# Taking eight unused columns off a small scratch tensor, so that every tensor laid behind it moves by 32 bytes

## The chip, the cores and the metric

The kernel runs on one core of a Trainium2 chip. The metric is the device time in microseconds (us) of one execution, as the median of several runs. The time before the change is 1901.88 us (three runs, 1901.18 to 1902.07).

## The reference

One layer of an encoder on 256 tokens of width 2048, in float32. Shortened:

```
x = x + 0.5 * swiglu_ffn(x, ffn1_norm, ffn1_w_in, ffn1_w_out)      # 2048 -> 2 x 5632 -> 2048
proj = rms_norm(x, mix_norm) @ w_in                                # 2048 -> 6144
# 8 heads of dilated attention and 8 heads of differential attention on proj
mixed = concatenate([a_o, b_o])
x = x + mixed @ w_out                                              # 2048 -> 2048
x = x + 0.5 * swiglu_ffn(x, ffn2_norm, ffn2_w_in, ffn2_w_out)

def swiglu_ffn(x, g, w_in, w_out):
    gate, up = split(rms_norm(x, g) @ w_in)
    return (silu(gate) * up) @ w_out
```

## The kernel before

All five big products have one form. The 256 tokens are held transposed, with the contraction in the 128 partitions, as TensorE's stationary operand. The weights stream from HBM through `w_raw` and are the moving operand, 512 columns at a time. To keep float32 accuracy, each operand is held as two parts, a rounded one (`_hi`) and the rest (`_lo`), and each product is three matmuls: line 330 multiplies the activations' `_hi` with `w_hi`, line 331 the same with `w_lo`, and line 332 the activations' `_lo` with `w_hi`. ScalarE makes `w_hi` from `w_raw` (line 531), VectorE makes `w_lo` from `w_raw` and `w_hi` (line 734), in a ring of four slots, so that TensorE, ScalarE and VectorE follow each other by semaphores.

The stationary operand is `h_hi`/`h_lo` for the up-projections of both feed-forward parts and for `w_in`; it is `act_hi`/`act_lo` for both down-projections, and `mix_hi`/`mix_lo` for `w_out`. In time: first feed-forward part to 794 us (its down-projection from 506 us), `w_in` with the attention of earlier heads slipped between its matmuls, `w_out` from about 1058 us, then the second feed-forward part, whose down-projection ends the kernel.

`inverse_root` (lines 744 to 760) computes 1/sqrt on VectorE by an integer estimate and three Newton steps. Its scratch tensor is `root`: the mean goes to columns 0 to n, a square to 16 to 16 + n, the bits to 32 to 32 + n, and n is at most 16.

How the tensors lie in on-chip memory matters for this change. They are laid one behind another in each partition, in the order in which the code asks for them, each start rounded up to a multiple of 32 bytes; `act_hi`, `act_lo` and the attention's tensors share one region, since they live at different times. Worked out from the shapes, with the first tensor `x_sb` at byte 1152:

| tensor | starts at byte | remainder by 128 |
|---|---|---|
| `rows` | 17536 | 0 |
| `h_hi`, `h_lo` | 33920, 50304 | 0 |
| `w_raw`, `w_hi`, `w_lo` | 66688, 99456, 115840 | 0 |
| `cst` | 132224 | 0 |
| `rstd`, `lam`, `root` | 138784, 138816, 138848 | 32, 64, 96 |
| `act_hi`, `act_lo` | 139072, 184128 | 64 |
| `mix_hi`, `mix_lo` | 139072, 155456 | 64 |
| `qkv` | 171840 | 64 |
| `qk_t`, `w_t` | 210752, 212800 | 64 |
| `head_ss`, `head_rstd` | 215872, 215904 | 64, 96 |
| `qk_ss`, `qk_rstd` | 217472, 217536 | 0, 64 |

Slices of `act`, `mix` and `h` that TensorE loads are 512 bytes long and lie at multiples of 512 bytes from the tensor's start.

Inside the attention, GpSimd multiplies and rotates queries and keys (lines 1005 to 1014), and TensorE transposes and multiplies per head (lines 414, 427, 436, 448).

Of the kernel before, what the change touches and what calls it, by code (L numbers as in the profile page):

```python
# [25 lines left out]
P = 128  # L26
# [81 lines left out]
def hybrid_layer_kernel(nc, x, ffn1_norm, ffn1_w_in, ffn1_w_out, mix_norm, w_in, a_q_norm, a_k_norm, b_q_norm,  # L108
# [8 lines left out]
    with ExitStack() as ctx:  # L117
        def sb(name, shape, dt=F32, stack=ctx):
            return stack.enter_context(nc.sbuf_tensor(name, shape, dt))
# [16 lines left out]
        sumsq = sb("sumsq", [P, TT, 4])  # L136
        rstd = sb("rstd", [P, TT])
        lam = sb("lam", [P, 4])
        root = sb("root", [P, 56])


        with ExitStack() as hidden:
# [893 lines left out]
```

How the kernel before makes its waits and increments, by code:

```python
        def wait_read(eng, stage, q):  # L236
            b, before = place(stage, q)
            eng.wait_ge(bank_free[b], READS[stage][b] + before + 1)
# [20 lines left out]
        @block.sync  # L260
# [1 line left out]
            def load(src, col, k0, count, p, j):  # L262
                if not isinstance(p, int) or p >= RAW:
                    sp.wait_ge(lo_ready, (p - RAW + 1) * 2)
                sp.dma_start(w_raw[:, j % RAW, 0:count, :],
                             src[:, k0:k0 + count, bass.ds(col, NC)]).then_inc(raw_landed[j % RAW], 16)
# [5 lines left out]
            def ffn(w1, w2, s_in, s_out, started, gain, norms):  # L273
                gate_up = tiled(w1)
                with sp.Fori(started, FFN_ITERS) as i:
                    load_chunk(gate_up, i * NC, PARTS_D, i * 8 + PIECE[s_in])
                    load_chunk(gate_up, i * NC + FF, PARTS_D, i * 8 + PIECE[s_in] + 4)
                if gain is not None:
                    sp.wait_ge(rows_ready, norms)
                    sp.dma_start(gain_row[:, :], gain.to_broadcast([P, D])).then_inc(gain_landed, 16)
                down = tiled(w2)
                with sp.Fori(0, 4) as n:
                    load_chunk(down, n * NC, PARTS_F, n * len(PARTS_F) + PIECE[s_out])
# [22 lines left out]
                for kind in range(3):  # L306
                    load_chunk(qkv_w, base + kind * (D // 2), PARTS_D, PIECE[QKV] + SEG * g + 4 * kind)
            sp.wait_ge(rows_ready, ROWS[R_MIX])
            sp.dma_start(gain_row[:, :], ffn2_norm.to_broadcast([P, D])).then_inc(gain_landed, 16)
```

## Time and profile before

| what | value |
|---|---|
| median of 3 runs | 1901.88 us |
| profiled execution, its own time | 1901.88 us |
| its span, first to last instruction | 1899.8 us |
| mean granted clock of TensorE | 0.998 of full speed |
| TensorE busy | 1878.3 us, 99% of the span |
| VectorE busy | 1021.0 us, 54% |
| ScalarE busy | 857.3 us, 45% |
| GpSimd busy | 60.1 us, 3% |
| traffic | 352.86 MB, mean 186 GB/s |

The span is what the trace can be asked about; the profiled execution's own time is 2.1 us more. A matmul's duration in the profile overlaps with that of the next, because the engine is a pipeline. How fast TensorE goes is therefore read from the distance between the starts of matmuls that follow each other, not from the duration of one.

### The profile page before, as it was taken

The page shows a single profiled execution, that of the slowest core. Times are in us where ns is not written, and L with a number is a line of the kernel's source. Part 1 is how long each engine was busy: PE and PEld are TensorE (multiplying, and loading weights), DVE is VectorE, ACT ScalarE, POOL GpSimd, SP SyncE. Part 2 cuts the span into 40 slices and gives each one's busy share as a digit, 9 for nine tenths or more (in the row PEclk, how much of TensorE's full clock was granted, in tenths as well). Part 3 has the DMA queues.
Part 4 walks back from the last instruction along what each step waited for, and adds up shares of the span by engine and source line. Part 5 has one row for each costly group of instructions (what it writes and reads, how often), then busy time and mean ns, then how long its engine had stood idle before and what let it go on. Part 6 is the DMA issues. An engine that isn't in the chain of part 4 may idle for free.

```text
span 1899.8 us, 22606 instructions
## 1 busy us (share of the span) xinstructions
PE 1878.3 (99%) x8528; PEld 1553.5 (82%) x8528; DVE 1021.0 (54%) x1142; ACT 857.3 (45%) x1063; POOL 60.1 (3%) x60
## 2 busy tenths in 40 slices
PE   7999999999999999999999999999999999999999
PEld 6888888888888888877888788888888888888887
DVE  5544445444544554667777666444444454444443
ACT  5444444444434444555555554444444444433342
POOL 0000000000000000122021100000000000000000
PEclk9999999999999999999999999999999999999999
DMA  8555555555655565554545355555555555555563
GB/s 304 187 191 191 184 197 180 197 182 193 207 188 173 190 201 191 183 190 137 178 155 184 127 171 179 183 198 180 195 186 189 192 184 197 180 180 186 198 206 116
DMA packets 178135, 352.86 MB, mean 186 GB/s; under 512 B 6561, under 2 KB 7201, under 8 KB 177825
## 3 DMA queue, kind: packets, MB, share of 16 engines
q1 hardware_dynamic: 177936, 352.07, 54.3%
q8 instruction: 35, 0.57, 0.1%
q14 instruction: 20, 0.16, 0.0%
q10 hardware_dynamic: 144, 0.07, 0.0%
HBM read 350.01 MB, written 2.10 MB: 185 GB/s over the span
## 4 chain that ended last, share of the span: by engine, by line
PE 94%; DVE 3%; ACT 1%; issue 1%; POOL 1%; DMA 0%; SPq 0%; ACTq 0%
PE acc L330 30%; PE acc L332 30%; PE acc L331 30%; DVE w_lo L734 1%; PE turn L357 1%; PE turn L427 1%; PE turn L448 1%; DMA w_raw<-in_ffn_w_in 0%; ACT w_hi L531 0%; PE turn L332 0%; PE turn L330 0%; PE turn L331 0%; ACT probs L621 0%; PE turn L436 0%; PE turn L414 0%
## 5 line engine op out<-in xcount | busy, mean ns | idle before, releaser
L734 DVE TENSOR_TENSOR w_lo<-w_raw,w_hi 128x1024 fp32r<-128x1024 f32 (+1 forms) x672 | 821.2, 1227 | 845.6 <-ACT w_hi L531 844.1
L531 ACT ACTIVATE w_hi<-w_raw 128x1024 fp32r<-128x1024 f32 (+1 forms) x672 | 697.2, 1040 | 974.8 <-PE acc L332 952.5
L330 PE MATMUL acc<-w_hi,h_hi 128*128 128x512 f32 x1792 | 703.2, 392 | 1.9 <-DVE w_lo L734 1.9
L332 PE MATMUL acc<-w_hi,h_lo 128*128 128x512 f32 x1792 | 698.3, 390 | 0.0
L331 PE MATMUL acc<-w_lo,h_hi 128*128 128x512 f32 x1792 | 698.1, 390 | 0.0
L330 PEld LDWEIGHTS acc<-w_hi,h_hi 128*128 128x128 f32 x1792 | 336.9, 188 | 73.3 <-issue 4.9
L332 PEld LDWEIGHTS acc<-w_hi,h_lo 128*128 128x128 f32 x1792 | 336.8, 188 | 70.4
L331 PEld LDWEIGHTS acc<-w_lo,h_hi 128*128 128x128 f32 x1792 | 337.0, 188 | 68.6
L330 PE MATMUL acc<-w_hi,act_hi 128*128 128x512 f32 x704 | 277.2, 394 | 0.0
L332 PE MATMUL acc<-w_hi,act_lo 128*128 128x512 f32 x704 | 276.0, 392 | 0.0
L331 PE MATMUL acc<-w_lo,act_hi 128*128 128x512 f32 x704 | 273.7, 389 | 0.0
L332 PEld LDWEIGHTS acc<-w_hi,act_lo 128*128 128x128 f32 x704 | 132.2, 188 | 30.3
L331 PEld LDWEIGHTS acc<-w_lo,act_hi 128*128 128x128 f32 x704 | 132.2, 188 | 29.4
L330 PEld LDWEIGHTS acc<-w_hi,act_hi 128*128 128x128 f32 x704 | 132.3, 188 | 26.7
L1005 POOL TENSOR_TENSOR qkv<-qkv,gains 128x1024 f32<-128x1024 f32 x8 | 26.5, 3306 | 992.6 <-DVE qkv L853 992.6
L357 PE MATMUL turn<-cst,rows 128*128 128x128 f32 x272 | 37.1, 281 | 8.8 <-DVE rows L773 8.8
L357 PEld LDWEIGHTS turn<-cst,rows 128*128 128x128 f32 x272 | 33.0, 145 | 13.3 <-issue 7.9
L330 PE MATMUL acc<-w_hi,mix_hi 128*128 128x512 f32 x96 | 39.9, 415 | 0.0
L332 PE MATMUL acc<-w_hi,mix_lo 128*128 128x512 f32 x96 | 38.4, 400 | 0.0
L331 PE MATMUL acc<-w_lo,mix_hi 128*128 128x512 f32 x96 | 38.1, 397 | 0.0
L782 DVE SCALAR_TENSOR_TENSOR rows<-acc,rstd,rows 128x512 f32<-128x512 f32 x44 | 30.9, 743 | 0.0
L550 ACT ACTIVATE rows<-acc,rstd 128x512 f32<-128x512 f32 x44 | 27.5, 674 | 0.0
(88 smaller groups left out, 594.6 us busy)
## 6 DMA issues: line engine op xcount, KB each, us to landing
w_raw<-in_ffn_w_in SPq DMA_DIRECT2D x176, 1024.0 KB, 4.9
w_raw<-in_ffn_w_out SPq DMA_DIRECT2D x64, 1024.0 KB, 5.0
w_raw<-in_w_in SPq DMA_DIRECT2D x48, 1024.0 KB, 5.2
w_raw<-in_ffn_w_out SPq DMA_DIRECT2D x32, 768.0 KB, 4.2
w_raw<-in_w_out SPq DMA_DIRECT2D x16, 1024.0 KB, 5.0
x_sb<-in_x SPq DMA_DIRECT2D x4, 512.0 KB, 7.9
out_y<-x_sb SPq DMA_DIRECT2D x4, 512.0 KB, 6.4
gain_row<-in_ffn_norm SPq DMA_DIRECT2D x4, 256.0 KB, 8.5
```

Source lines behind the costliest of these rows:

```text
L330: nc.tensor.matmul(o, hi, w_hi[:, slot, kk, :], start=first and kk == 0, stop=False)
L331: nc.tensor.matmul(o, hi, w_lo[:, slot, kk, :], start=False, stop=False)
L332: mm = nc.tensor.matmul(o, lo, w_hi[:, slot, kk, :], start=False, stop=last and kk == count - 1)
L357: mm = nc.tensor.transpose(turn4[pair][:, k, t * P:(t + 1) * P], rows[:, buf, t, k * P:(k + 1) * P], ident)
L427: mm = nc.tensor.matmul(score[:, c, t, :], qk_t[part, 0, t * P:(t + 1) * P], qk_t[part, 1, :], start=True, stop=True)
L448: mm = nc.tensor.matmul(head_acc[:, t, :], w_t[:, kt, t * P:(t + 1) * P], qkv[:, g % 2, 2, kt, n * HD:(n + 1) * HD], start=kt == 0, stop=k ...
L531: nc.scalar.activation(w_hi[:, v % RING, 0:count, :], w_raw[:, v // 2 % RAW, k0:k0 + count, :], ACT.Copy).then_inc(hi_ready, 1)
L550: s = nc.scalar.activation(rows[:, 0, t, :], acc[0][:, t, :], ACT.Silu, scale=rstd[:, t:t + 1])
L734: nc.vector.tensor_tensor(w_lo[:, v % RING, 0:count, :], w_raw[:, v // 2 % RAW, k0:k0 + count, :], w_hi[:, v % RING, 0:count, :].bitcast(F32),
L782: s = nc.vector.scalar_tensor_tensor(rows[:, 0, t, :], acc[1][:, t, :], rstd[:, t:t + 1], rows[:, 0, t, :], ALU.mult, ALU.mult)
L1005: link(nc.gpsimd.tensor_tensor(whole, whole, gain.unsqueeze(1).to_broadcast([P, TT * heads, width]), ALU.mult))
```

## The change

`root` gets 48 columns in place of 56. Columns 48 to 55 are read and written by nothing. Everything that is asked for behind `root` starts 32 bytes earlier. `act_hi` and `mix_hi` start at byte 139040, `act_lo` at 184096, `mix_lo` at 155424, `qkv` at 171808, `w_t` at 212768. No instruction is added, removed or moved.

```
         rstd = sb("rstd", [P, TT])
         lam = sb("lam", [P, 4])
-        root = sb("root", [P, 56])
+        root = sb("root", [P, 48])
```

## Rows read from the trace of the kernel before

**Rows 1.** The page's first part: busy time, share of the span, instructions.

```profile
PE 1878.3 (99%) x8528; PEld 1553.5 (82%) x8528; DVE 1021.0 (54%) x1142; ACT 857.3 (45%) x1063; POOL 60.1 (3%) x60
```

**Rows 2.** The chain that ended last, its shares by line.

```profile
by line: PE acc L330 29.8%; PE acc L332 29.7%; PE acc L331 29.6%; DVE w_lo L734 1.5%; PE turn L357 1.5%; issue 0.7%; PE turn L427 0.6%; PE turn L448 0.6%; DMA w_raw<-in_ffn_w_in 0.5%; ACT w_hi L531 0.5%; PE turn L332 0.4%; PE turn L330 0.4%
```

**Rows 3.** Waits over the whole kernel: total us, times, longest us.

```profile
ACT w_hi L531 <- PE acc L332: 952.5, 615, 3.6
DVE w_lo L734 <- ACT w_hi L531: 844.1, 581, 6.7
```

**Rows 4.** TensorE in order of time, up-projection: first and last of 19 starts.

```profile
460.17 0.39 PE L330 MATMUL acc<-w_hi,h_hi 128*128 128x512 f32 x1
...
464.25 0.39 PE L330 MATMUL acc<-w_hi,h_hi 128*128 128x512 f32 x1
```

**Rows 5.** The same, first down-projection: first and last of 22 starts.

```profile
599.77 0.39 PE L330 MATMUL acc<-w_hi,act_hi 128*128 128x512 f32 x1
...
604.58 0.39 PE L330 MATMUL acc<-w_hi,act_hi 128*128 128x512 f32 x1
```

**Rows 6.** The same, second down-projection: first and last of 22 starts.

```profile
1834.75 0.39 PE L330 MATMUL acc<-w_hi,act_hi 128*128 128x512 f32 x1
...
1839.56 0.39 PE L330 MATMUL acc<-w_hi,act_hi 128*128 128x512 f32 x1
```

**Rows 7.** The same, output projection: first and last of 9 starts.

```profile
1101.98 0.39 PE L330 MATMUL acc<-w_hi,mix_hi 128*128 128x512 f32 x1
...
1103.81 0.39 PE L332 MATMUL acc<-w_hi,mix_lo 128*128 128x512 f32 x1
```

**Rows 8.** Groups by line and shape: line 330's matmuls, and its weight loads (PEld).

```profile
L330 PEld LDWEIGHTS acc<-w_hi,h_hi 128*128 128x128 f32 x1792 | 336.9, 188 | 73.3 <-issue 4.9
...
L330 PE MATMUL acc<-w_hi,act_hi 128*128 128x512 f32 x704 | 277.2, 394 | 0.0
...
L330 PEld LDWEIGHTS acc<-w_hi,act_hi 128*128 128x128 f32 x704 | 132.3, 188 | 26.7
...
L330 PE MATMUL acc<-w_hi,mix_hi 128*128 128x512 f32 x96 | 39.9, 415 | 0.0
...
L330 PE MATMUL turn<-w_hi,mix_hi 128*128 128x512 f32 x32 | 12.9, 403 | 0.0
```

**Rows 9.** The same view, VectorE and ScalarE on tensors with different starts.

```profile
L536 ACT ACTIVATE h_hi<-turn 128x1024 fp32r<-128x1024 f32 x12 | 12.1, 1011 | 8.7 <-PE turn L357 8.7
...
L536 ACT ACTIVATE mix_hi<-turn 128x1024 fp32r<-128x1024 f32 x4 | 4.0, 1008 | 0.0
...
L754 DVE SCALAR_TENSOR_TENSOR root<-root 128x16 f32<-128x16 f32 x12 | 2.1, 176 | 0.4
L755 DVE SCALAR_TENSOR_TENSOR qk_rstd<-root,qk_rstd 128x16 f32<-128x16 f32 x12 | 2.1, 175 | 0.4
...
L755 DVE SCALAR_TENSOR_TENSOR qk_rstd<-root,qk_rstd 128x8 f32<-128x8 f32 x12 | 2.0, 167 | 0.4
...
L755 DVE SCALAR_TENSOR_TENSOR head_rstd<-root,head_rstd 128x8 f32<-128x8 f32 x9 | 1.5, 167 | 0.3
```

**Rows 10.** Stretches around the end of `w_in`: busy time per engine, granted clock.

```profile
1048.00:1056.00 8.00, 5.51 (x25) 4.21 (x23) 5.83 (x6) 3.32 (x10) 6.09 (x7) 0.99 0.40 126
1056.00:1063.00 7.00, 6.21 (x20) 5.26 (x21) 1.86 (x3) 2.59 (x5) 0.00 (x0) 0.53 0.44 157
```

**Rows 11.** The timeline of the same stretch.

```profile
1047.33 3.31 POOL L1005 TENSOR_TENSOR qkv<-qkv,gains 128x1024 f32<-128x1024 f32 x1 [12.04 <-DVE qkv L853]
1048.30 3.42 DVE L734 TENSOR_TENSOR w_lo<-w_raw,w_hi 128x1024 fp32r<-128x1024 f32 x1
...
1053.12 0.39 PE L332 MATMUL acc<-w_hi,h_lo 128*128 128x512 f32 x1
...
1056.79 1.11 PE L436 MATMUL turn<-cst,probs 128*128 128x128 f32 x4 [3.28 <-DVE row_inv L879]
```

**Rows 12.** The chain in order of time: one matmul behind that stop.

```profile
1060.04 0.43 PE acc L330
```

## Prediction

> **What bounds the kernel now.** I read the page's first part, then the chain, then the waits, and last the matmuls in order of time. The first part shows TensorE busy for 1878.3 of 1899.8 us, VectorE for little more than half of the span [rows 1]. A share of 99% could still hide short waits, so the chain comes next: three lines, 330 to 332, carry 89.1% of it [rows 2]. The waits say the same from the other side. ScalarE waited 952.5 us for TensorE to give a ring slot back, and VectorE 844.1 us for ScalarE; TensorE is on neither left side [rows 3]. So outside a few places in the attention the time is the number of matmuls times the distance between their starts, and only what changes that distance, or stops TensorE, can change the time.
>
> That distance differs by stage, although the matmuls have the same shape. With `h` as the stationary operand it is (464.25 - 460.17)/18 = 226.7 ns [rows 4]. With `act` it is (604.58 - 599.77)/21 = 229.0 ns, in the second feed-forward part again (1839.56 - 1834.75)/21 = 229.0 ns [rows 5, 6]. With `mix` it is (1103.81 - 1101.98)/8 = 228.8 ns [rows 7]. The excess is 2.3 ns for each matmul. The moving operand, the clock and the pace of the other engines are the same. What differs is where the stationary operand lies: `h` begins at a multiple of 128 bytes, `act` and `mix` 64 bytes past one, and they also lie in the upper part of the memory. The trace can't tell these two readings apart, and the change bears on the first alone.
>
> **The change part by part.** It removes no instruction, adds none and adds no wait: 0 us. Columns 48 to 55 of `root` have no reader or writer, since n is at most 16 and the last slice ends at 48: 0 us. What is left is the move by 32 bytes, which takes everything behind `root` from a multiple of 64 to 32 past one. `w_raw`, `w_hi`, `w_lo`, `h`, `rows`, `x_sb` and `cst` lie ahead of it and stay. So the up-projections and `w_in` keep their 226.7 ns, and the weights' DMAs, `w_hi` and `w_lo` are as before.
>
> *TensorE's loads of `act` and `mix`.* The down-projections have 3 x 704 = 2112 such matmuls, the output projection 3 x (96 + 32) = 384, together 2496 [rows 8]. If the 2.3 ns come from the start 64 bytes past a multiple of 128, they are worth 2496 x 2.3 ns = 5.7 us now. A start 32 bytes past could keep that step, lose it, or pay a second one. The bounds are therefore -5.7 us and +5.7 us. I take 0. A load takes 188 ns from `h` as from `act` [rows 8], so the start of 64 past doesn't show in the load's own record, and it has 229.0 - 188 = 41 ns before it would reach the next matmul. Were a load cut into eight pieces of 64 bytes, a ninth, which the new start would touch, would cost 188/8 = 23.5 ns, inside these 41. If it weren't hidden it would cost 2496 x 23.5 ns = 58.7 us. I leave that out of the range, because the operand's present start shows a step of a tenth of that at most.
>
> The Trainium skill ("TensorE: Matmul & The Clock Gate", Step-by-step: what each phase is for) says that TensorE reads SBUF by two independent ports, one for the moving operand and one for weight loads, so that a load takes nothing from a running matmul. By it the place of `act` can't matter while a load fits behind a matmul, and the sum would be 0 for the move, as I take it; but the 2.3 ns above are a difference that it doesn't account for. The Trainium skill ("SBUF — State Buffer", Operand start alignment) asks only that an operand start at a multiple of its element's size, and says that its runs timed nothing.
>
> *ScalarE, VectorE and GpSimd.* Their reads and writes of `act`, `mix` and the attention's tensors move as well. The nearest rows compare starts that differ. ScalarE writes `h_hi` (remainder 0) in 1011 ns and `mix_hi` (64) in 1008. VectorE takes 176 ns for `root` into `root` (96, so 32 past a multiple of 64) and 175 for `qk_rstd`, a multiple of 64; at eight columns `head_rstd` (96) and `qk_rstd` (64) take 167 ns each [rows 9]. No large tensor shows a start 32 bytes past a multiple of 64, so these small ones are the only rows on it, and they say 0. A slowdown here would first be taken up by the 952.5 and 844.1 us of waiting above [rows 3]. That cover is gone in the attention, at one place above all.
>
> *The stop at the end of `w_in`.* GpSimd's multiplication of `qkv` at 1047.33 takes 3.31 us, and `w_lo` beside it 3.42 us. TensorE starts its last matmul at 1053.12 and the next work at 1056.79 [rows 11]. Behind this stop the granted clock is 0.53 of full speed from 1056 to 1063, and 0.99 in the stretch ahead [rows 10]; matmuls start 0.43 us apart at the lower level (1.2 GHz) [rows 12] and 0.23 us at the upper one (2.4 GHz) [rows 4]. The clock row gives about 0.47 x 7 = 3.3 us lost to it. With the same durations this comes back unchanged, so 0 us. If the cover is gone, GpSimd's longer work lengthens the stop one for one, and what is late next is the transposes of line 436 and everything behind them.
>
> Sum: 0 + 0 + 0 = 0 us against the profiled execution's span of 1899.8 and its own time of 1901.88, which is also the median. The forecast is 1901.9 us.
>
> **The rivals.**
>
> *No gain, a second step (slower).* The loads of `act` and `mix` begin 32 past a multiple of 64, each 512-byte slice now ends in the middle of such a piece, and the distance grows by the same 2.3 ns again. For it: the existing excess goes with a start that is no multiple of 128, and 32 is the smaller alignment. Against it: the load's 188 ns don't differ between 0 and 64. Time: 1901.9 + 5.7 = 1907.6. It decides from 1.5 ns for each matmul on (3.8 us over 2496).
>
> *The step falls away (faster).* The excess belongs to the particular distance between the stationary and the moving operand's places, which is 64 by remainder now and 32 after. Then `act` and `mix` could run at 226.7 ns, and 5.7 us are won: 1896.2. Nothing in the rows speaks for 32 being better than 64; only that both distances are unlike zero.
>
> *The stop moves.* An attention engine that is a few tens of ns slower or faster on moved tensors shifts the stop at 1053, and the fall of the clock behind it vanishes (-3.3 us, to 1898.6) or a second one appears at another attention stop (+3.3 us, to 1905.2). For it: one such fall is there. Against it: no row shows a duration that depends on the start.
>
> *The change does nothing at all.* Had the rounding of starts swallowed the eight columns, nothing would have moved. But 32 bytes are just one rounding unit and `root` ends at 139040, so `act_hi` does move. It gives the same time as the forecast.
>
> **How the numbers follow.** A measurement of this kernel can tell about 0.2%, 3.8 us, from no change: the three runs spread over 0.9 us. No change in time, with `act` and `mix` at 229 ns: 0.60. Second step: 0.23. Step gone: 0.10. Stop moved: 0.07, with 0.03 slower and 0.04 faster, taken as just over the bound together with small shifts. That makes faster 0.14, same 0.60, slower 0.26. The range reaches to the second step with a little more for the clock, 1909, and down to the step gone, 1896. Outside are dearer straddling loads and both effects together, under 2 in 10. The likeliest case alone would be 1900.5 to 1903.5.
>
> **What would show it.** In the changed profile the instruction counts are those of [rows 1]. Right is a distance of 229 ns in the down-projections and in the output projection, and 226.7 in the up-projections, where nothing moved; weight loads at 188 ns; one fall of the clock, near 1056. A distance of 231 ns or more, or 227 or less, in the down-projections proves the alignment rivals, and then the up-projections must not have changed. If the distance is the same and the time isn't, the stops in the attention are the place to look. The prediction is wrong if a start 32 bytes past a multiple of 64 costs any engine on TensorE's path more than 1.5 ns for each of its 2496 operations.

## The result, and the profile after

The changed kernel takes 1914.14 us (median of 4 runs, 1910.89 to 1914.24), the kernel before in the same comparison 1901.91 us (4 runs). The ratio is 1.0058, with a 95% interval of 1.0046 to 1.0070: 0.6% slower. The forecast was no change, and the time lies above the stated range.

The profiled execution of the changed kernel has a span of 1908.7 us, 8.9 us more than before. The same 22606 instructions are there. First the page's busy times, which answer to [rows 1]:

```profile
PE 1887.2 (99%) x8528; PEld 1551.3 (81%) x8528; DVE 1021.0 (53%) x1142; ACT 857.5 (45%) x1063; POOL 60.1 (3%) x60
```

The waits, as in [rows 3]:

```profile
ACT w_hi L531 <- PE acc L332: 962.0, 615, 2.2
DVE w_lo L734 <- ACT w_hi L531: 853.2, 588, 4.0
```

TensorE is busy for 8.9 us longer, which is the whole difference. VectorE, ScalarE and GpSimd are busy as long as before to within 0.2 us. ScalarE waits 9.5 us longer for TensorE, and VectorE 9.1 us longer for ScalarE. So no engine became slower but TensorE. Next, TensorE's matmuls in order of time, in the up-projection (22 starts shown by first and last), the first down-projection (23), the end of the output projection (47) and the second down-projection (23), as in [rows 4 to 7]:

```profile
459.73 0.39 PE L332 MATMUL acc<-w_hi,h_lo 128*128 128x512 f32 x1
...
464.49 0.39 PE L332 MATMUL acc<-w_hi,h_lo 128*128 128x512 f32 x1
...
599.68 0.40 PE L332 MATMUL acc<-w_hi,act_lo 128*128 128x512 f32 x1
...
604.81 0.39 PE L330 MATMUL acc<-w_hi,act_hi 128*128 128x512 f32 x1
...
1157.05 0.40 PE L331 MATMUL acc<-w_lo,mix_hi 128*128 128x512 f32 x1
...
1167.78 0.39 PE L332 MATMUL acc<-w_hi,mix_lo 128*128 128x512 f32 x1
...
1834.74 0.39 PE L330 MATMUL acc<-w_hi,act_hi 128*128 128x512 f32 x1
...
1839.88 0.39 PE L331 MATMUL acc<-w_lo,act_hi 128*128 128x512 f32 x1
```

With `h` the distance is 4.76/21 = 226.7 ns, as before. With `act` it is 5.13/22 = 233.2 and 5.14/22 = 233.6 ns, where it was 229.0. With `mix` it is 10.73/46 = 233.3 ns. The same 47 starts in the kernel before:

```profile
1153.09 0.39 PE L331 MATMUL acc<-w_lo,mix_hi 128*128 128x512 f32 x1
...
1163.62 0.40 PE L332 MATMUL acc<-w_hi,mix_lo 128*128 128x512 f32 x1
```

They are 10.53/46 = 228.9 ns apart. A start is read to 0.01 us, so a distance over some 22 matmuls is good to about 0.5 ns.

The weight loads' own record says nothing of it. In the groups by line and shape a load from `act` takes 188 ns, exactly as in [rows 8], and the ScalarE and VectorE groups of [rows 9] are the same to within 1 ns too:

```profile
L330 PEld LDWEIGHTS acc<-w_hi,act_hi 128*128 128x128 f32 x704 | 132.2, 188 | 31.6
...
L536 ACT ACTIVATE mix_hi<-turn 128x1024 fp32r<-128x1024 f32 x4 | 4.0, 1008 | 0.0
...
L754 DVE SCALAR_TENSOR_TENSOR root<-root 128x16 f32<-128x16 f32 x12 | 2.1, 176 | 0.4
```

Is it TensorE alone, or do the other engines' and the DMAs' accesses to the memory get in its way? The last 28 matmuls of the kernel answer this, since nothing else is left to do. In the changed kernel the stretch has (busy PE, PEld, DVE, ACT, POOL, then the granted clock and the DMA share):

```profile
1897.50:1903.80 6.30, 6.30 (x28) 5.07 (x27) 0.00 (x0) 0.00 (x0) 0.00 (x0) 1.00 0.00 0
```

The 28 starts from 1897.51 to 1903.81 are 6.30/27 = 233.3 ns apart. In the kernel before, the last 28, from 1888.77 to 1894.95, are 6.18/27 = 228.9 ns apart, again with the others idle. So the extra time is there with no other engine and no DMA at work beside TensorE.

The lengths of the stages, each from its first big matmul to that of the next stage:

| stage | before, us | changed, us | difference |
|---|---|---|---|
| first up-projection | 491.4 | 491.9 | +0.4 |
| first down-projection | 245.2 | 249.9 | +4.7 |
| `w_in` with attention | 307.2 | 306.5 | -0.6 |
| `w_out` | 105.4 | 105.1 | -0.3 |
| second up-projection | 488.7 | 488.7 | 0.0 |
| second down-projection, to the last matmul | 242.4 | 247.1 | +4.7 |

Each down-projection carries 4.7 us, or 4.4 ns for each of 1056 matmuls. The two stages in the middle are a little shorter although `mix` is slower, because TensorE's clock didn't fall there in this execution. The same stretches as in [rows 10], with one column each for busy PE, PEld, DVE, ACT, POOL, then the granted clock:

```profile
1048.00:1056.00 8.00, 8.00 (x41) 6.79 (x40) 7.56 (x17) 3.33 (x8) 3.33 (x2) 1.00 0.45 158
1056.00:1063.00 7.00, 3.75 (x22) 2.94 (x21) 4.83 (x7) 4.13 (x8) 3.44 (x6) 1.00 0.46 151
```

The stop is there, only later, and the clock stays at 2.4 GHz behind it (1.00). In the timeline, TensorE starts the last matmul ahead of it at 1058.41 and the next work at 1062.06, 3.65 us, against 3.67 in [rows 11]:

```profile
1058.41 0.39 PE L332 MATMUL acc<-w_hi,h_lo 128*128 128x512 f32 x1
...
1062.06 0.66 PE L436 MATMUL turn<-cst,probs 128*128 128x128 f32 x4 [3.25 <-DVE row_inv L879]
```

That fall of the clock comes and goes from one execution to the next of the same kernel. Further executions of the changed kernel lie at 1911 to 1912.5 us, where the mean granted clock is 0.999 or 1.000, and near 1914 us, where it is 0.998. The kernel before, run 14 times in a later comparison, spreads from 1898.96 to 1902.27 us.

### The profile page after: what moved, and what is told of

It reads as the page before. It is cut to its first block, busy times and chain, and to the rows that moved or that the text cites. A ratio compares the mean times of both kernels' runs of the same rounds, so it can differ in the third digit from the quotient of the medians.

```text
span 1908.7 us, 22606 instructions
## 1 busy us (share of the span) xinstructions
PE 1887.2 (99%) x8528; PEld 1551.3 (81%) x8528; DVE 1021.0 (53%) x1142; ACT 857.5 (45%) x1063; POOL 60.1 (3%) x60
## 4 chain that ended last, share of the span: by engine, by line
PE 94%; DVE 3%; ACT 1%; issue 1%; POOL 1%; DMA 0%; SPq 0%; ACTq 0%
PE acc L332 30%; PE acc L331 30%; PE acc L330 30%; DVE w_lo L734 1%; PE turn L357 1%; PE turn L427 1%; PE turn L448 1%; DMA w_raw<-in_ffn_w_in 0%; ACT w_hi L531 0%; PE turn L332 0%; PE turn L331 0%; PE turn L330 0%; ACT probs L621 0%; PE turn L436 0%; DVE qk_ss L846 0%
## 5 line engine op out<-in xcount | busy, mean ns | idle before, releaser
L332 PE MATMUL acc<-w_hi,act_lo 128*128 128x512 f32 x704 | 280.6, 399 | 0.0
```

Source lines behind the costliest of these rows:

```text
L332: mm = nc.tensor.matmul(o, lo, w_hi[:, slot, kk, :], start=False, stop=last and kk == count - 1)
```

## Experiments

All kernels differ from the kernel before only in where tensors lie: in unused columns, and in one case also in the place of `cst` in the order. The theories' letters are those of the expectations. D below is the start of the stationary operand (`h`, `act` or `mix`) less the start of the moving one (`w_hi`), modulo 256 bytes, written from -96 to 128. The `_lo` tensors have the same remainder as their `_hi` partners unless said. The kernel before has D = 0 for `h` and -64 for `act` and `mix`; the changed one has -96 for the latter.

**First group: is it the stationary operand's own place?**

72 columns in `root`, so `act` and `mix` start at a multiple of 128 bytes:

```
-        root = sb("root", [P, 56])
+        root = sb("root", [P, 72])
```

> `root` has 72 columns, so `act` and `mix` start at a multiple of 128 bytes, like `h`, still in the upper part of the memory. Theory A (the start of the stationary operand by 128 bytes sets the distance between matmuls): the distance with `act` falls from 229.0 to 226.7 ns, and the time by 2496 x 2.3 ns = 5.7 us to about 1896. Theory C (the excess of 2.3 ns comes with the upper part of the memory, and only 32 bytes off a multiple of 64 costs extra): 229.0 ns and 1901.9 us. Theory D (the loss sits in the attention's tensors, not in `act` and `mix`): 229.0 ns in the down-projections.

Measured 1896.85 us (10 runs) against 1901.65 (14 runs), ratio 0.9975 (0.9965 to 0.9984). The down-projection in order of time, 23 starts:

```profile
599.81 0.39 PE L330 MATMUL acc<-w_hi,act_hi 128*128 128x512 f32 x1
...
604.80 0.39 PE L331 MATMUL acc<-w_lo,act_hi 128*128 128x512 f32 x1
```

4.99/22 = 226.8 ns: the excess of `act` over `h` is gone. The place was its cause, not the upper part of the memory (theory C falls), and not the attention's tensors (theory D falls). This version beats both kernels.

The same with 64 columns:

> `root` has 64 columns, so `act` and `mix` start 96 bytes past a multiple of 128: again 32 past a multiple of 64, but shifted the other way than in the changed kernel. Theory A with a fold by 64: the same 233.3 ns as the changed kernel and 1911 to 1914 us. If the two halves of 128 bytes differ: something between 229.0 and 233.3 ns, or more. Theory C: 233.3 ns.

Measured 1911.37 us (4 runs), ratio 1.0052 (1.0037 to 1.0068). 5.13/22 = 233.2 ns in the down-projection, the changed kernel's distance.

Eight columns between `act_hi` and `act_lo`:

```
+            pad = sb("pad", [P, 8], F32, hidden)
             act_lo = sb("act_lo", [P, KF, SEQ], F32R, hidden)
```

> The kernel before with eight unused columns between `act_hi` and `act_lo`: only `act_lo` moves, to 96 past a multiple of 128; `mix` and the attention stay. Theory A, each load pays for itself: one load of three is dearer, so the distance rises by a third of the 4.4 ns, to about 230.4 ns, and the time by 2112 x 1.5 ns = 3.1 us to 1905. If the extra comes only where two neighbouring loads have different starts, it is more than a third. If it is the attention's tensors that cost: no change, 1901.9.

Measured once, 1909.88 us, with 5.13/22 = 233.2 ns. One moved load in three costs as much as three. So a load doesn't pay for itself; the reading that each of the 2496 loads has a price of its own is wrong.

Sixteen columns ahead of `w_hi`:

```
+        pad = sb("pad", [P, 16])
         w_hi = sb("w_hi", [P, RING, UK, NC], F32R)
```

> The kernel before with 16 unused columns ahead of `w_hi`: `w_hi` and `w_lo` start 64 past a multiple of 128, `act` and `mix` at a multiple of 128, `h` stays at a multiple. Theory A (only the stationary operand counts): `h` 226.7 ns, `act` 226.7 ns, about 1896 us. Theory B (the place of the stationary operand relative to the moving one counts): `h` rises to 229.0 ns and `act` stays at 229.0, so 5376 x 2.3 = 12 us slower, 1914.

Measured once, 1910.80 us. The up-projection, 23 starts:

```profile
459.81 0.39 PE L331 MATMUL acc<-w_hi,h_hi 128*128 128x512 f32 x1
...
464.85 0.39 PE L332 MATMUL acc<-w_lo,h_hi 128*128 128x512 f32 x1
```

`h` hasn't moved, and its matmuls are 5.04/22 = 229.1 ns apart in place of 226.7. `act`, now at a multiple of 128, has 5.03/22 = 228.6. The stationary operand's own place (theory A) explains neither.

**Second group: the distance between both operands?**

Both moved by 64 bytes against `h`:

```
+        pad = sb("pad", [P, 16])
         w_hi = sb("w_hi", [P, RING, UK, NC], F32R)
...
-        root = sb("root", [P, 56])
+        root = sb("root", [P, 72])
```

> `w_hi` and `w_lo` start 64 past a multiple of 128 and so do `act` and `mix`; `h` stays at a multiple of 128. Theory B (only the distance between the two operands' places counts): `act` 226.7 ns, `h` 229.0. Theory E (each operand's own start counts, and the worse of the two sets the pace): `h` 229.0 and `act` 229.0, about 1911 us. Theory F (the costs of the two operands add up): `act` 231.2 ns, about 1916.

Measured once, 1908.09 us. The down-projection (24 starts):

```profile
599.78 0.39 PE L332 MATMUL acc<-w_lo,act_hi 128*128 128x512 f32 x1
...
604.99 0.39 PE L331 MATMUL acc<-w_hi,act_hi 128*128 128x512 f32 x1
```

`act` 5.21/23 = 226.5 ns, `h` 5.27/23 = 229.1 ns. Both operands of the down-projection start 64 past a multiple of 128 and run at the best distance. Only theory B gives that.

`act_hi` and `act_lo` at two different distances, with `root` at 64 columns and 24 columns ahead of `act_lo` (D = -32 for `act_hi` and `mix`, +64 for `act_lo`):

> `act_hi` and all of the attention's tensors start 96 past a multiple of 128, `act_lo` stays at 64. Two of three loads of a down-projection move, where the run before moved one and saw the full 4.3 ns. If one such load in three is enough for the whole step: 233.3 ns again in the down-projections and in `mix`, about 1911 us. If what counts is a mixture of starts (64 and 96): 233.3 here as well, but then both must be told from the changed kernel, where the three loads agree and the distance is 233.3 too; so 233.3 speaks for the first reading.

Measured once, 1908.00 us, `act` 5.32/23 = 231.3 ns. Neither reading gave this. Each of the two distances by itself gives 233.2 to 233.6 ns (below). How two different distances within a triple combine stays open.

Only the attention's tensors and `mix` moved (eight columns ahead of `mix_hi`; this moves them up by 32 bytes, to D = -32 for `mix`, where the change moves them down, to -96):

> Only `mix` and the attention's own tensors move by 32 bytes, `act` stays. If the loss is TensorE's loads: `act` 229.0 ns, `mix` 233.3, and 384 x 4.4 ns = 1.7 us more, 1903.6, apart from the fall of the clock near 1055. If ScalarE, VectorE or GpSimd lose time on moved tensors: longer stops between 820 and 1060, and more than 3 us.

Measured once, 1900.57 us, span 1898.7. `act` 5.04/22 = 229.1 ns. The end of the output projection, 47 starts:

```profile
1151.78 0.39 PE L332 MATMUL acc<-w_lo,mix_hi 128*128 128x512 f32 x1
...
1162.51 0.39 PE L333 MATMUL acc<-w_hi,mix_lo 128*128 128x512 f32 x1
```

`mix` has 10.73/46 = 233.3 ns, as was expected of the loads. The stretch that had the fall of the clock in [rows 10]:

```profile
1056.00:1063.00 7.00, 6.09 (x35) 5.36 (x36) 2.98 (x4) 4.77 (x11) 0.00 (x0) 1.00 0.52 172
```

The clock is at 1.00 here, so about 3.3 us fell away, and the rest is 1898.7 - 1899.8 + 3.3 = +2.2 us, near the 1.7 that the loads of `mix` were to cost. The stop ahead of it isn't longer (3.6 us in place of 3.67).

The moving operand off by 32 bytes, all else at multiples of 128 (eight columns ahead of `w_hi`, `root` at 64 columns):

> `w_hi` and `w_lo` start 32 past a multiple of 128; `h`, `act` and `mix` start at multiples of 128. The moving operand takes part in all 7872 big matmuls. Theory E: each runs at 233.3 ns in place of 226.7 (`h`) and 229.0 (`act`), so 5376 x 6.6 + 2496 x 4.4 ns = 46 us slower, about 1948. If only the stationary operand's 32 bytes cost, and the moving operand costs no more than the 2.3 ns it showed at 64: about 1911.

Measured once, 1944.25 us, 43 us above the kernel before in the same comparison (1901.39). Here D = -32 everywhere:

```profile
459.69 0.39 PE L332 MATMUL acc<-w_lo,h_hi 128*128 128x512 f32 x1
...
464.83 0.39 PE L333 MATMUL acc<-w_hi,h_lo 128*128 128x512 f32 x1
```

`h` has 5.14/22 = 233.6 ns.

**Third group: absolute place, period, grain.**

Everything moved by 32 bytes (eight columns ahead of `x_sb`):

> Eight unused columns ahead of the first tensor: everything moves by 32 bytes, so `h`, `w_hi` and `w_lo` start 32 past a multiple of 128 and `act`, `mix` 96 past one. The distances between the operands' places are those of the kernel before. Theory B (only the distance between the two operands counts): `h` 226.7, `act` 229.0 ns, the time of the kernel before, 1899 to 1902 us. Theory G (an operand that starts off a multiple of 64 is read dearly by itself): `h` and `act` at 233.3 ns or more, at least 1944 us.

Measured once, 1900.82 us: `h` (24 starts from 459.64 to 464.86) 5.22/23 = 227.0, `act` 5.27/23 = 229.1 ns. None of the operands starts at a multiple of 64 any more, and nothing is lost. The operands' own starts are without effect here; theory G falls.

`cst` laid first, `root` at 72 columns:

```
+        cst = sb("cst", [P, N_CONST])
         x_sb = sb("x_sb", [P, TT, D])
...
-        cst = sb("cst", [P, N_CONST])
...
-        root = sb("root", [P, 56])
+        root = sb("root", [P, 72])
```

> `cst` is laid ahead of everything and `root` has 72 columns: `h`, `w_hi` and `w_lo` start at multiples of 512 bytes, `act` and `mix` at multiples of 128. Theory B by 128 bytes: the same as with 72 columns alone, 226.7 ns in both and 1894 to 1898 us. If a larger period than 128 bytes plays a part: `h` below or above 226.7 ns, 5376 matmuls, so 5.4 us for each ns.

Measured 1910.16 us (5 runs), ratio 1.0044 (1.0031 to 1.0058), where theory B by 128 bytes gave 1894 to 1898. The down-projection:

```profile
599.72 0.39 PE L332 MATMUL acc<-w_hi,act_lo 128*128 128x512 f32 x1
...
604.83 0.39 PE L330 MATMUL acc<-w_hi,act_hi 128*128 128x512 f32 x1
```

5.11/22 = 232.3 ns, although both operands start at multiples of 128; `h` has 5.21/23 = 226.5. D is 128 by 256 here, and was 0 by 256 in the first experiment. The theory stood, its period didn't.

`w_hi` and `w_lo` 16 bytes past a multiple of 128, by a slice that starts inside a wider tensor:

> `w_hi` and `w_lo` begin 16 bytes past a multiple of 128, `h` at a multiple, `act` and `mix` 64 past one: distances of 16 bytes (`h`) and 48 (`act`). Theory B with a grain of 64 bytes: neither is a multiple of 64, so 233.3 ns in both, about 1945 us. With a grain of 32 bytes: a distance of 16 is dearer than one of 32, above 233.3 ns.

Measured once, 1932.14 us: `h` 5.31/23 = 230.9 ns, `act` 5.13/22 = 233.2. The expectation reckoned the distances by 128 bytes. By 256 the run mixes two: `w_hi` starts at byte 99472 and `w_lo` at 115984, which is 16512 or 64.5 times 256 behind it. `h` has D = -16 against `w_hi` but +112 against `w_lo`, and `act` has +48 and -80. So no value of D stands by itself here, and the run doesn't tell where between 0 and -32 the price begins. Both readings of the expectation gave 233.3 ns or more for `h`; neither came true, and neither was tested cleanly.

Only `act` moved by 32 bytes, the counterpart of the run with the attention alone (eight columns ahead of `act_hi`; again up, to D = -32, where the change goes down, to -96):

> The kernel before with `act_hi` and `act_lo` moved by 32 bytes and everything else in place: the other half of the change. The down-projections lengthen by 4.65 and 4.7 us as in the changed kernel, `mix` stays, and 1901.9 becomes about 1911.2, or 1908 where the clock doesn't fall near 1055 us. If the loss needs the attention's tensors, it stays at 1902.

Measured once, 1909.70 us, span 1907.7 with the clock at 1.000 throughout; `act` 5.13/22 = 233.2 ns. The down-projections' loss comes back at full size without the attention's tensors.

**Fourth group: sign and period.**

> `root` with 88 columns: `act` and `mix` lie 64 bytes past the place that is a multiple of 256 away from `w_hi` (D = +64; D is -64 in the kernel before and -96 in the changed one). If only the size of D counts: 229.0 ns and 1899 to 1902 us. If its sign counts too: another distance, from 226.7 to 233.4 ns, which is 1896 to 1914 us.

Measured once, 1910.37 us: 5.14/22 = 233.6 ns at D = +64, against 229.0 at -64. The sign counts.

> 32 unused columns ahead of `w_hi`: D = -128 for `h`, -64 for `act` and `mix` as before. With a period of 256 bytes, which is how I now read the run at multiples of 512: `h` at 232.4 ns, 5376 x 5.7 ns = 31 us slower, 1932. With a period of 128 (and the reordering of `cst` as the cause in that run): `h` 226.7 ns and 1902.

Measured once, 1927.06 us. `cst` keeps its place among the tensors here:

```profile
459.71 0.39 PE L331 MATMUL acc<-w_hi,h_hi 128*128 128x512 f32 x1
...
464.82 0.39 PE L332 MATMUL acc<-w_lo,h_hi 128*128 128x512 f32 x1
```

5.11/22 = 232.3 ns for `h`, as `act` had with `cst` laid first. So the period isn't 128. The distances that are 0 by 256 measured so far are both cheap, and one of them (39680 bytes, for `act` with 72 columns) is an odd multiple of 256, the other (65536, for `h`) a multiple of 512. So no period of 512 or more is needed.

> `root` with 80 columns: D = +32 for `act` and `mix`. If the size of D counts: 233.3 ns as at D = -32, 1908 to 1912 us. If D has to be a multiple of 64 to be cheap: the same. If the sign counts: less than 233.3.

Measured once, 1913.87 us: 5.13/22 = 233.2 ns at D = +32.

All of it in one table:

| D by 256 | distance of matmuls, ns | seen in |
|---|---|---|
| 0 | 226.5 to 227.0 | `h` before; `act` with 72 columns; `act` with both moved |
| -32 | 233.2 to 233.6 | `act` with 64 columns; `act` alone moved; `mix` alone moved; `h`, moving operand at 32 |
| -64 | 228.6 to 229.1 | `act` before; `h` and `act`, moving operand at 64 |
| -96 | 233.2 to 233.6 | `act` and `mix`, changed kernel |
| 128 | 232.3 | `act` with `cst` first; `h`, moving operand at 128 |
| +32, +64 | 233.2 to 233.6 | `act`, 80 columns; `act`, 88 columns |
| -16 with `w_hi`, +112 with `w_lo` | 230.9 | `h`, moving operand at 16 |
| +48 with `w_hi`, -80 with `w_lo` | 233.2 | `act`, moving operand at 16 |
| -64 for `act_hi`, -32 for `act_lo` | 233.2 | `act_lo` alone moved |
| -32 for `act_hi`, +64 for `act_lo` | 231.3 | `act_hi` and `act_lo` moved apart |

## Why the prediction was wrong, point by point

*What bounds the kernel.* Right. TensorE's busy time took all of the 8.9 us, and the number of matmuls times their distance gives the stages' lengths.

*The excess of 2.3 ns with `act`.* It was seen, and it was the right thing to look at, but read wrongly. I tied it to where `act` begins by itself. It comes from the distance between the two operands' places, since `h` gets it too when only `w_hi` moves, and loses nothing when all moves together.

*The price of moving `act` and `mix`: the step that failed.* I took 0 between bounds of -5.7 and +5.7 us, on the ground that a load's record shows 188 ns at either start. It shows 188 ns at 226.7 as at 233.2 ns of distance, so it was no evidence on this, and the 41 ns reckoned as free behind a load hid nothing. The term is 2112 x 4.4 = 9.3 us in the down-projections (9.4 by the stages) and 384 x 4.4 = 1.7 us for `mix`, together 11.0 us. The upper bound assumed a second step as large as the first, 2.3 ns, and the step is 4.4. The dependence isn't one that grows with misalignment: of the seven values of D that were measured by themselves, the kernel before happened to sit on the second best, so most moves lead up from there. Why the distance between the places matters inside TensorE isn't shown; that it needs no other engine is, by the last 28 matmuls.

The Trainium skill ("TensorE: Matmul & The Clock Gate", Step-by-step: what each phase is for) has weight loads and the moving operand on read ports of their own, so that a load takes nothing from a running matmul. By it no place could matter; the runs here, from 226.5 to 233.6 ns on instructions that are the same, speak against it.

*The rivals.* The slower one, a second step in the same place, had the right stages and the right sign, and half the size. The faster one named the distance between the two operands, which is the cause, but not how the time depends on it: -96 isn't better than -64.

*ScalarE, VectorE, GpSimd.* Right: no duration in the rows compared changed, and moving the attention alone left the stop as long as it was.

*The stop at the end of `w_in`.* Its length held (3.67 and 3.65 us). The prediction had GpSimd on the path through it. But in [rows 11] it is VectorE's `row_inv` that releases TensorE, and no run here made GpSimd slower, so that part wasn't tested. That the clock's fall behind the stop "comes back unchanged" didn't hold for every execution. It was absent in the profiled one, and by the two groups of run times it is worth about 3 us.

*The whole difference.* The two medians compare like with like: three of the four runs behind 1914.14 have a mean granted clock of 0.998, as the execution of 1901.88 us before has. So the fall isn't in the 12.2 us between them, of which the loads explain 11.0. The two profiled executions give the same once the fall is put back: 8.9 us and the 3.3 that it cost before are 12.2. The remaining 1.2 us weren't traced. Of these, 0.4 us lie in the first up-projection, where nothing moved and which varies by more than 1 us between these kernels (491.1 to 492.6), and most of the rest in the two middle stages.

*Nothing else moves.* Right: 226.7 ns with `h`, and the second up-projection is as long as before to within 0.1 us.

## What to carry to other kernels

Where TensorE is the bound, read the distance between the starts of its matmuls stage by stage; instructions of one shape at two distances are a finding by themselves, and a record of equal durations doesn't refute it. Here the places of stationary and moving operand should differ by a multiple of 256 bytes: 16 more unused columns in a scratch tensor won 0.25% over the kernel before and some 0.8% over the changed one. A tidy-up that frees no needed room can move every tensor behind it, so fix the starts of matmul operands rather than leave them to the order of allocation.

## What the hardware showed that I had not expected

- The place of one operand relative to the other sets the pace of float32r matmuls of 512 columns with a load of 128 columns each: 226.7 ns at D = 0 to 233.6 ns, 3%. Moving all operands together by 32 bytes costs nothing. The price is the same while every other engine and the DMAs are idle (233.3 ns over the last 28 matmuls).
- D = -64 is cheap (229.0 ns) and +64 isn't (233.6 ns). One load of three at another D is enough for the whole price (-64 with -32: 233.2 ns), but -32 with +64 gave 231.3 ns, less than either alone. Why is open; no run looked inside a load.
- Values between by themselves, and the same question for other types and widths, weren't tried.
